# Dealing an adaLN product and half of an output projection over the steps of an attention, and a sum of squares ahead of another adaLN product

## The chip, the core and the metric

One NeuronCore of a Trainium2 chip runs the whole program. The metric is device microseconds per execution, lower is better. All arrays are float32. The engines are TensorE (PE; weight loads are shown apart as PEld), VectorE (DVE), ScalarE (ACT), GpSimd (POOL) and SyncE (SP), which issues the large DMAs.

## The reference

Two residual layers over 256 positions of width 1024. Layer 0 has a mixer of differential and sparse attention, layer 1 a mixer of block attention (8 heads of 64, at this length plain causal attention) beside a diagonal state-space model (S5) with a gated linear unit (GLU). After each mixer comes a mixture of 32 SwiGLU experts. adaLN makes from the vector `c` six rows of 1024 numbers per layer: shift, scale and gate of the mixer, shift, scale and gate of the experts.

```python
mod = c_act @ ada_w[l] + ada_b[l]
sh1, sc1, g1, sh2, sc2, g2 = jnp.split(mod, 6, axis=-1)
h = rms_norm(x) * (1.0 + sc1[:, None, :]) + sh1[:, None, :]
# odd mixer
z = h @ w_in
cq, ck, cv, u = _split(z, ODD_SPLIT)
cq = apply_rope(rms_norm(cq.reshape(bsz, seq, C_HEADS, HEAD_DIM), c_qn), cos_h, sin_h)
ck = apply_rope(rms_norm(ck.reshape(bsz, seq, C_HEADS, HEAD_DIM), c_kn), cos_h, sin_h)
o_c = moba_attention(cq, ck, cv)
y = jax.nn.gelu(s5_scan(u, ...))
y = y * jax.nn.sigmoid(y @ glu_w + glu_b)
y = jnp.concatenate([o_c, y], axis=-1) @ w_out
x = x + g1[:, None, :] * y
h = rms_norm(x) * (1.0 + sc2[:, None, :]) + sh2[:, None, :]
x = x + g2[:, None, :] * hier_moe(h, ...)
```

## The kernel before

Each engine runs one list of instructions, written by hand, and waits on semaphores that the others raise; no scheduler moves anything. The 256 tokens are two tiles `t` of 128. `xT` and `hT` hold the residual and the modulated input with the 1024 features on partitions in 8 blocks `k`; `htok` holds rows by token, and serves as scratch for squares.

All weights come through `ring`, six slots of 2 MB, in one fixed order (`LOADS0`, the 96 expert loads of layer 0, `LOADS1`, 96 expert loads of layer 1). SP issues a load (L439) when the slot's former user has told that it is done, for the mixers through `slot_used`, for the experts through the semaphore of the expert's matmuls.

PSUM has eight banks: `A4` (four), `B4` and `B5` (together `OB`), `B6` and `B7` (`TRB`). Everything that passes through `TRB` is a pass with a name in `ORDER`, PE fills one of the two banks, ACT copies it out (`passed`, `tr_evac`, `ada_evac`), and `pass_bank` makes PE wait for the bank of two passes ago.

An adaLN third `ada{l}r{r}` is 2048 of a layer's 6144 numbers: `ada_part` (L530) multiplies the replicated `crep` (128x32 stationary) with eight half slots of weights, four column groups into the four 32-partition strips of one bank, 32 matmuls in all. A float32 matmul of the program stands as two records in the trace, so a third is 64 records, two `k` of it are 16. ACT copies the bank to `modrow`, and four transposes (`ada{l}c{r}`, L519) and one more copy turn the row into columns `modc`.

The second mixer runs like this on PE: first the half of third 1 (`ada1r1`), the column sums of squares of `xT` (`sum_squares`, L561, into `B5`), the other half. DVE then makes the norm (`norm_modulate`, from L1077 to L1088) and raises `h_ready`. PE projects the S5 input (L983), then `s5_input`, `s5_output` and `project1` (L591) alternate with the scans on DVE. `gated_unit` (L971) fills `B4` and `B5`, ACT makes its sigmoid (L1853, `sig_ready`). `c_norm` on DVE normalizes and rotates q and k of one token tile (it needs a square root from ACT, `root`, L1656) and tells `qk_ready`; the passes `C0` to `C3` (L519) transpose them. Third 2 (`ada1r2`, `ada1c2`) stands between `C1` and `C2`.

`attention` has eight units: `t` 0 and 1, and four pairs of heads each. A step `j` issues the scores of unit j (`att_score`, L606, two 64-row matmuls into half of `A4`), the transposes of its probabilities `LAG_PT` steps later (`att_pt`, L519) and the product with v `LAG_PV` steps later (`att_pv`, L628, into `OB[t]`). DVE scales and masks (L1043), takes the maximum (L1138) and negates it (L1040); ACT exponentiates each of two heads (L1669) and copies the transposed probabilities (L1644). Then `out_proj(1, 1)`, the half of the output projection that takes the S5 rows `hT[:, 4:8]` (DVE L1603, `yo_ready`), fills all of `A4` (L659); `oC0` and `oC1` transpose the attention rows; `out_proj(1, 0)` adds their half, followed block by block by residual, squares and their column sums. The expert stage `moe(1)` begins with the norm, the routing and the packing (L714), then its experts (L742 gate and up, L759 down, L769 combination).

Of the kernel before, what the change touches and what calls it, by code (L numbers as in the profile page):

```python
# [120 lines left out]
def build(nc, a, cst_d, out_d):  # L121
    ctx = ExitStack()
    with ctx:
# [170 lines left out]
        ada_done = sem("ada_rows_done")  # L294
# [82 lines left out]
        LAG_PT, LAG_PV = 3, 4  # L377
# [10 lines left out]
        for j in range(N0 + LAG_PT):  # L388
            if 0 <= j - LAG_PT < N0:
                ORDER.append(f"p{j - LAG_PT}")  # L390
            if j == ADA1_COLS_AT:
                ORDER.append("ada1c0")
        ORDER += ["oB0", "oB1", "oA0", "oA1", "bt0", "bt1", "bt2", "bt3", "ct0", "ct1", "k0", "h0_0", "h0_1", "h0_2", "h0_3", "ada1r1", "ada1c1",
                  "C0", "C1", "ada1r2", "ada1c2", "C2", "C3"]
        ORDER += [f"p{N0 + j}" for j in range(N1)] + ["oC0", "oC1", "h1_0", "h1_1", "h1_2", "h1_3"]
# [101 lines left out]
        def _(pe):  # L497
# [134 lines left out]
            def attention(l, base, units, hook=None):  # L632

                n = len(units)
                for j in range(n + LAG_PV):
                    if j < n:
                        att_score(l, base, j, *units[j])
                    if 0 <= j - LAG_PT < n:
                        att_pt(base, j - LAG_PT, *units[j - LAG_PT])
                    if 0 <= j - LAG_PV:  # L640
                        if l == 1 and j == LAG_PV:
                            pe.wait_ge(sig_ready, 1)
                        if l == 0 and j - LAG_PV in (8, 12):
                            pe.wait_ge(o_ready, (j - LAG_PV) // 4 - 1)
                        att_pv(base, j - LAG_PV, *units[j - LAG_PV])
                    if hook:
                        hook(j)

            def out_proj(l, cc):


                n = n_of(l, "out", cc)
                full(n)
                if cc == 1:
                    pe.wait_ge(score_read, (N0, N0 + N1)[l])
                for b in range(4):
                    for k in range(4):
                        for f in (2 * b, 2 * b + 1):
                            ins = pe.matmul(A4[:, b, TOK * (f % 2):TOK * (f % 2) + TOK],  # L659
                                            slot4(n)[:, k, P * f:P * f + P], hT[:, 4 * cc + k, :],  # L660
                                            start=(cc == 1 and k == 0 and f % 2 == 0), stop=(cc == 0 and k == 3),
                                            skip_group_check=True)
                    if cc == 0:
                        ins.then_inc(wout_done, 1)
                        if b:
                            sum_squares(2 * l + 1, b - 1)
                if cc == 1:
                    ins.then_inc(slot_used, 1)
                else:
                    pe.wait_ge(wout_done, 4 * (l + 1))  # L670
                    pe.nop().then_inc(slot_used, 1)
                    sum_squares(2 * l + 1, 3)
# [241 lines left out]
            for s, name in ((1, "oB"), (0, "oA")):  # L914
# [4 lines left out]
                out_proj(0, s)  # L919
# [9 lines left out]
            pe.nop().then_inc(slot_used, 1)  # L929
# [68 lines left out]
            project1(5)  # L998
            gated_unit()
            for h in range(2):  # L1000
                tr_unit(f"C{h}", [z1[:, 0, 512 * h + P * b:512 * h + P * b + P] for b in range(4)], [(qk_ready, 7)])

            ada_rows(1, 2)
            ada_columns(1, 2)
            for h in range(2):
# [989 lines left out]
```

## Time and profile before

| | before |
|---|---|
| three executions, us | 1469.05, 1465.03, 1468.69 |
| median, us | 1468.69 |
| the profiled execution, us | 1468.64 |
| its span from first to last instruction, us | 1466.8 |
| PE busy, of the span | 1306.7 us, 89% |
| DVE busy | 429.8 us, 29% |
| ACT busy | 217.8 us, 15% |
| mean granted clock of PE | 0.936 of full |

The second mixer lies between 762 and 945 us of the span, the expert stages before and after it. Busy time of PE counts matmuls whose ends are modelled, and a matmul at half clock is busy for longer, so the share alone doesn't say what binds; the idle time before each row and its releaser do.

### The profile page before, as it was taken

Reading aid. Unit: us, or ns where it says so; the run is one execution under the profiler, and the core shown is the slowest. Engines: PE = TensorE matmul, PEld = TensorE weight load, DVE = VectorE, ACT = ScalarE, POOL = GpSimd, SP = SyncE. Lnnn points to the kernel's source line nnn. Section 1 sums busy time; section 2 is a strip of 40 time slices with the busy share of each in tenths; the row PEclk is TensorE's granted clock in tenths of the full one; section 3 lists DMA queues with packets and bytes.
Section 4 is the critical chain, followed back from the end, with each engine's and each line's share of the span. In section 5 each row is a group of like instructions: output and inputs, shape, how many; then the busy total and the mean of one; then the engine's idle time right before and its main releaser. Section 6 shows DMA issues by size and latency. Waiting matters only on the chain.

```text
span 1466.8 us, 15111 instructions
## 1 busy us (share of the span) xinstructions
PE 1306.7 (89%) x6161; PEld 653.0 (45%) x6161; DVE 429.8 (29%) x887; ACT 217.8 (15%) x458; POOL 104.0 (7%) x127
## 2 busy tenths in 40 slices
PE   5999988799898988989978989889989998999897
PEld 2444567643344433433335445664334333343333
DVE  3264567521111110211123954342112111111112
ACT  2121341211110110101010024011101010111110
POOL 2000202100300300300000000000000000000000
PEclk9999859899999999999998997979999999999999
DMA  9987713079999999999998256308999999999993
GB/s 370 379 329 301 275 49 115 0 317 429 428 428 427 427 427 428 428 427 428 428 421 316 113 203 261 115 1 332 427 428 428 428 427 428 427 428 428 428 428 147
DMA packets 51769, 493.45 MB, mean 336 GB/s; under 512 B 4712, under 2 KB 5936, under 8 KB 20848
## 3 DMA queue, kind: packets, MB, share of 16 engines
q1 hardware_dynamic: 48816, 488.33, 80.3%
q10 hardware_dynamic: 1856, 3.20, 0.6%
q0 software_dynamic: 1024, 0.88, 0.3%
q8 instruction: 54, 0.88, 0.2%
q14 instruction: 19, 0.16, 0.0%
HBM read 489.24 MB, written 3.15 MB: 336 GB/s over the span
## 4 chain that ended last, share of the span: by engine, by line
PE 54%; DMA 34%; DVE 7%; issue 3%; ACT 1%; SPq 1%; DVEq 0%; POOLq 0%; POOL 0%; PEldq 0%; ACTq 0%
DMA ring<-in_moe_w 32%; PE B L742 22%; PE B L575 6%; PE B L759 5%; PE A L659 4%; PE B L530 3%; PE A L769 3%; PE B L714 2%; DMA ring<-in_ada_w 2%; PE B L591 2%; PE B L519 1%; PE B L628 1%; PE B L983 1%; DVE hT L1088 1%; PE B L686 1%
## 5 line engine op out<-in xcount | busy, mean ns | idle before, releaser
L742 PE MATMUL B<-ring,work 128*64 128x512 f32 x2048 | 477.6, 621 | 60.0 <-DMA ring<-in_moe_w 57.4
L742 PEld LDWEIGHTS B<-ring,work 128*64 128x64 f32 x2048 | 160.6, 142 | 339.1 <-issue 337.7
L759 PE MATMUL B<-ring,work 128*64 128x512 f32 x1024 | 231.9, 594 | 1.2 <-ACT work L1706 1.2
L1319 DVE TENSOR_TENSOR work<-work,B 64x512 f32<-64x512 f32 x64 | 68.3, 1067 | 496.2 <-ACT work L1702 495.8
L759 PEld LDWEIGHTS B<-ring,work 128*64 128x64 f32 x1024 | 76.6, 137 | 136.6 <-issue 136.6
L1702 ACT ACTIVATE work<-B 64x512 f32<-64x512 f32 x64 | 37.7, 589 | 621.4 <-PE B L742 621.4
L769 PE MATMUL A<-work 128*128 128x256 f32 x512 | 118.1, 384 | 8.9 <-DVE work L1325 8.9
L769 PEld LDWEIGHTS A<-work 128*128 128x128 f32 x512 | 94.7, 190 | 28.4 <-issue 16.9
L1926 POOL COPY work<-work 128x512 f32 x62 | 38.1, 614 | 901.0 <-PE B L742 744.5
L575 PE MATMUL B<-ring,hT 128*128 128x512 f32 (+1 forms) x224 | 94.6, 582 | 4.4 <-DVE hT L1088 3.3
L1325 DVE COPY work<-B 64x512 f32<-64x512 f32 x64 | 43.7, 683 | 117.3 <-PE B L759 117.3
L575 PEld LDWEIGHTS B<-ring,hT 128*128 128x128 f32 x224 | 43.6, 197 | 52.9 <-issue 48.2
L1710 ACT COPY work<-B 64x512 f32<-64x512 f32 x64 | 37.2, 581 | 194.5 <-PE B L759 194.5
L530 PE MATMUL B<-ring,crep 128*32 128x512 f32 x384 | 48.7, 658 | 17.3 <-issue 9.5
L1315 DVE COPY work<-B 128x512 f32<-128x512 f32 x16 | 11.1, 691 | 173.1 <-PE B L733 173.1
L659 PE MATMUL A<-hT,ring 128*128 128x256 f32 x256 | 56.9, 381 | 2.2 <-ACT hT L1644 2.2
L659 PEld LDWEIGHTS A<-hT,ring 128*128 128x128 f32 x256 | 48.3, 190 | 9.3 <-ACT hT L1644 2.9
L749 PEld LDWEIGHTS B<-cst,work 128*128 128x128 f32 x256 | 26.9, 141 | 50.3 <-issue 50.3
L591 PE MATMUL B<-ring,hT 128*128 128x512 f32 x96 | 45.0, 625 | 0.0
L749 PE MATMUL B<-cst,work 128*128 128x128 f32 x256 | 41.9, 286 | 0.0
L714 PE MATMUL B<-work,htok 128*128 128x256 f32 x128 | 33.8, 430 | 8.8 <-DVEq L1046 8.8
L530 PEld LDWEIGHTS B<-ring,crep 128*32 128x32 f32 x384 | 13.5, 119 | 48.3 <-issue 38.9
(251 smaller groups left out, 916.5 us busy)
## 6 DMA issues: line engine op xcount, KB each, us to landing
ring<-in_moe_w SPq DMA_DIRECT2D x192, 2048.0 KB, 19.4
ring<-in_ada_w SPq DMA_DIRECT2D x24, 2048.0 KB, 18.2
ring<-in_ev_w_in SPq DMA_DIRECT2D x6, 2048.0 KB, 11.9
ring<-in_od_w_in SPq DMA_DIRECT2D x4, 2048.0 KB, 16.1
ring<-in_ev_w_out SPq DMA_DIRECT2D x2, 2048.0 KB, 7.6
ring<-in_od_w_out SPq DMA_DIRECT2D x2, 2048.0 KB, 7.6
s_tables<-hT ACTq DMA_DIRECT2D x8, 256.0 KB, 9.6
ring<-s_tables SPq DMA_DIRECT2D x1, 2048.0 KB, 25.5
```

The source lines that it names most:

```text
L530: ins = pe.matmul(bank[32 * g:32 * g + 32, :], crep[:, k, :], slot_rows(n)[:, k % 2, 512 * g:512 * g + 512], start=(k == 0), stop=(k == KD ...
L575: ins = pe.matmul(bank[:, 0:w], hT[:, k, P * t:P * t + P], slot8(n)[:, k, 0:w], start=(k == 0), stop=(k == KD - 1))
L591: ins = pe.matmul(OB[m != 5][:, :], hT[:, k, P * t:P * t + P], slot8(n)[:, k, :], start=(k == 0), stop=(k == KD - 1))
L659: ins = pe.matmul(A4[:, b, TOK * (f % 2):TOK * (f % 2) + TOK], slot4(n)[:, k, P * f:P * f + P], hT[:, 4 * cc + k, :], start=(cc == 1 and k ...
L714: ins = pe.matmul(bank[:, TOK * q:TOK * q + TOK], htok[:, t, P * f:P * f + P], Sp[:, t, TOK * h:TOK * h + TOK], start=(t == 0), stop=(t == 1))
L742: ins = pe.matmul(B5[64 * m:64 * m + 64, :], xs[:, k, :], w[:, k, :], start=(k == 0), stop=(k == KD - 1))
L749: ins = pe.transpose(B6[:, P * k:P * k + P], hid[:, q % 2, P * k:P * k + P], ident)
L759: ins = pe.matmul(B7[64 * m:64 * m + 64, :], hidTb[:, q % 2, k, :], w[:, k, 512 * m:512 * m + 512], start=(k == 0), stop=(k == KF - 1))
L769: ins = pe.matmul(A4[:, f // 2, TOK * (f % 2):TOK * (f % 2) + TOK], y2[:, pr % 2, P * f:P * f + P], SwT[:, g, pr % 2, :], start=False, sto ...
L1319: dve.tensor_tensor(hid[64:128, q % 2, :].rearrange("p (k q) -> p q k", k=KF), silu_a[64:128, q % 2, :].rearrange("p (q k) -> p q k", k=KF ...
L1325: dve.tensor_copy(y2[64 * (q % 2):64 * (q % 2) + 64, (q // 2) % 2, 0:512], B7[0:64, :]).then_inc(sm.y_lo, 1)
L1926: pool.tensor_copy(xge[:, e % 2], xgp[:, :, bass.ds(start, CH)]).then_inc(rows_ready, 1)
```

## The change

Only the second mixer changes.

- `sum_squares(2, b)` stands ahead of the whole of `ada1r1`.
- ACT takes `root(9)` ahead of the copy of projection 4 and `root(10)` ahead of that of projection 5. `C0` and `C1` stand ahead of the gated unit, on PE and on ACT.
- `ada1r2` is no pass through `TRB` any more: it is accumulated in `B5`, two `k` at each of the steps 1 to 4 of the attention, the first after `sig_ready`; ACT copies it at its step 5 (`ada_copied`), and `ada1c2` follows at step 6. The first product into `B5` of the attention (unit 4) waits for that copy.
- The lags of the second attention are 2 and 3 in place of 3 and 4.
- `out_proj` takes one block `b` of output columns a call. Blocks 0 to 2 of `out_proj(1, 1)` stand at the steps 8 to 10 of the attention, behind the last three products with v, block 3 after it. DVE makes `yo_ready` behind unit 5.

```diff
-        LAG_PT, LAG_PV = 3, 4
+        LAGS = [(3, 4), (2, 3)]
+        ADA2_COLS_AT = 6
...
-                        if l == 1 and j == LAG_PV:
-                            pe.wait_ge(sig_ready, 1)
+                        if l == 1 and j - lag_pv == 4:
+                            pe.wait_ge(ada_copied, 1)
...
-            def out_proj(l, cc):
+            def out_proj(l, cc, b, first):
                 n = n_of(l, "out", cc)
-                full(n)
-                if cc == 1:
-                    pe.wait_ge(score_read, (N0, N0 + N1)[l])
-                for b in range(4):
-                    for k in range(4):
+                if b == 0:
+                    full(n)
+                    if first:
+                        pe.wait_ge(score_read, (N0, N0 + N1)[l])
+                for k in range(4):
...
-            bank = pass_bank("ada1r1")
-            ada_part(bank, 1, 1, range(0, 4))
             for b in range(4):
                 sum_squares(2, b)
-            ada_part(bank, 1, 1, range(4, KD))
-            pe.nop().then_inc(tr_done, 1)
-            pe.nop().then_inc(slot_used, 1)
+            ada_rows(1, 1)
...
             project1(5)
+            for h in range(2):
+                tr_unit(f"C{h}", [...], [(qk_ready, 7)])
             gated_unit()
             for h in range(2):
-                tr_unit(f"C{h}", [...], [(qk_ready, 7)])
-
-            ada_rows(1, 2)
-            ada_columns(1, 2)
-            for h in range(2):
                 tr_unit(f"C{2 + h}", [...], [(qk_ready, 8)])
-            pe.wait_ge(tr_ev, U["C3"] + 1)
-            attention(1, N0, L1_UNITS)
-            pe.wait_ge(yo_ready, 1)
-            out_proj(1, 1)
+            pe.wait_ge(tr_ev, U["C1"] + 1)
+            def beside_c(j):
+                if j == 3:
+                    pe.wait_ge(tr_ev, U["C3"] + 1)
+                if 1 <= j <= 4:
+                    if j == 1:
+                        pe.wait_ge(sig_ready, 1)
+                    ada_part(B5, 1, 2, (2 * j - 2, 2 * j - 1))
+                if j == 4:
+                    pe.nop().then_inc(slot_used, 1)
+                if j == ADA2_COLS_AT:
+                    tr_unit("ada1c2", [...], [(ada_copied, 1)])
+                if j >= N1:
+                    if j == N1:
+                        pe.wait_ge(yo_ready, 1)
+                    out_proj(1, 1, j - N1, True)
+            attention(1, N0, L1_UNITS, beside_c)
+            out_proj(1, 1, 3, True)
...
             for j, (s, b, t) in enumerate(L1_UNITS):
                 softmax_unit(16, j, s, b, t, sc_sb1, prob1)
-            dve.wait_ge(gy_ready, 1)
-            dve.wait_ge(sig_ready, 1)
-            dve.tensor_tensor(hT[:, 4:8, :], gy, vv[:, 1], ALU.mult).then_inc(yo_ready, 1)
+                if j == 5:
+                    dve.wait_ge(gy_ready, 1)
+                    dve.wait_ge(sig_ready, 1)
+                    dve.tensor_tensor(hT[:, 4:8, :], gy, vv[:, 1], ALU.mult).then_inc(yo_ready, 1)
...
+            root(9, small[:, 0:16])
             c_evac(4)
-            root(9, small[:, 0:16])
+            root(10, small[:, 0:16])
             c_evac(5)
+            for h in range(2):
+                tr_evac(f"C{h}", qkT1[:, 4 * h:4 * h + 4, 0:P], 4)
             act.wait_ge(in_s5, 16 * N_S5)
             act.wait_ge(glu_done, 1)
             for f in range(4):
                 ins = act.activation(vv[:, 1, f, :], OB[f // 2][...], ACT.Sigmoid, bias=glub[:, f:f + 1])
             ins.then_inc(sig_ready, 1)
             for h in range(2):
-                tr_evac(f"C{h}", qkT1[:, 4 * h:4 * h + 4, 0:P], 4)
-            root(10, small[:, 0:16])
-            ada_evac(1, "r2")
-            ada_evac(1, "c2")
-            for h in range(2):
                 tr_evac(f"C{2 + h}", qkT1[:, 4 * h:4 * h + 4, P:2 * P], 4)
+            def beside_c(j):
+                if j == 5:
+                    act.wait_ge(ada_done, 6)
+                    act.copy(modrow[:, :], B5[:, :]).then_inc(ada_copied, 1)
+                if j == ADA2_COLS_AT:
+                    ada_evac(1, "c2")
```

PE at the start of the second mixer, before (L530 is the adaLN product, L561 the sum of squares, L983 the first projection; a count is one of program matmuls):

```order
L408 COMPARE_AND_BRANCH
L530 MATMUL B<-ring,crep 32x512 x16
L561 MATMUL B<-htok,cst 128x256 x8
L530 MATMUL B<-ring,crep 32x512 x16
L983 MATMUL B<-hT,ring 128x256 x32
L939 MATMUL A<-work,BT 128x128 x16
```

The same place after (the same work has the lines L536, L567 and L985):

```order
L414 COMPARE_AND_BRANCH
L567 MATMUL B<-htok,cst 128x256 x8
L536 MATMUL B<-ring,crep 32x512 x32
L985 MATMUL B<-hT,ring 128x256 x32
L941 MATMUL A<-work,BT 128x128 x16
```

The eight matmuls of the sum of squares moved from the middle of the product to its front; nothing else is different there.

PE from the last projections to the first units of the attention, before (L971 the gated unit, L519 transposes, L606 scores, L628 products with v):

```order
L591 MATMUL B<-ring,hT 128x512 x16
L971 MATMUL B<-work,ring 128x256 x16
L519 MATMUL B<-cst,work 128x128 x8
L530 MATMUL B<-ring,crep 32x512 x32
L519 MATMUL B<-cst,modrow 128x128 x4
L519 MATMUL B<-cst,work 128x128 x8
L606 MATMUL A<-work 128x128 x8
L519 MATMUL B<-cst,work 128x128 x2
L606 MATMUL A<-work 128x256 x2
L519 MATMUL B<-cst,work 128x128 x2
L628 MATMUL B<-work 128x64 x2
```

After (L973, L525, L612, L634 for the same):

```order
L597 MATMUL B<-ring,hT 128x512 x16
L525 MATMUL B<-cst,work 128x128 x8
L973 MATMUL B<-work,ring 128x256 x16
L525 MATMUL B<-cst,work 128x128 x8
L612 MATMUL A<-work 128x128 x4
L536 MATMUL B<-ring,crep 32x512 x8
L612 MATMUL A<-work 128x128 x2
L525 MATMUL B<-cst,work 128x128 x2
L536 MATMUL B<-ring,crep 32x512 x8
L612 MATMUL A<-work 128x128 x2
L525 MATMUL B<-cst,work 128x128 x2
L634 MATMUL B<-work 128x64 x2
```

The transposes of the first token tile went ahead of the gated unit, and the 32 matmuls of the adaLN third became four lots of 8, each behind the scores of a unit.

PE at the end of the attention, before (L659 is the output projection, the last L519 the transposes of the attention rows):

```order
L519 MATMUL B<-cst,work 128x128 x4
L628 MATMUL B<-work 128x64 x4
L519 MATMUL B<-cst,work 128x128 x4
L628 MATMUL B<-work 128x64 x8
L659 MATMUL A<-hT,ring 128x256 x32
L519 MATMUL B<-cst,htok 128x128 x8
```

After (L664 is the output projection):

```order
L525 MATMUL B<-cst,work 128x128 x4
L634 MATMUL B<-work 128x64 x4
L664 MATMUL A<-hT,ring 128x256 x8
L525 MATMUL B<-cst,work 128x128 x4
L634 MATMUL B<-work 128x64 x4
L664 MATMUL A<-hT,ring 128x256 x8
L634 MATMUL B<-work 128x64 x4
L664 MATMUL A<-hT,ring 128x256 x16
L525 MATMUL B<-cst,htok 128x128 x8
```

The last two products with v now stand between blocks of the output projection, and the last half of it stands between the last product and the transposes of the rows.

## Rows read from the trace of the kernel before

**Rows 1.** The page, part 4: chain of work that ended last.

```profile
PE 54%; DMA 34%; DVE 7%; issue 3%; ACT 1%; SPq 1%; DVEq 0%; POOLq 0%; POOL 0%; PEldq 0%; ACTq 0%
```

**Rows 2.** Windows: stretch, length, busy time by engine, PEclk, DMA share, GB/s.

```profile
774.00:776.00 2.00, 2.00 (x12) 0.46 (x8) 0.00 (x0) 0.00 (x0) 0.00 (x0) 0.50 1.07 415
776.00:778.00 2.00, 2.00 (x17) 0.50 (x10) 0.00 (x0) 0.00 (x0) 0.00 (x0) 0.79 1.05 430
...
790.00:792.00 2.00, 2.00 (x7) 1.60 (x6) 1.93 (x4) 0.00 (x0) 0.00 (x0) 0.62 1.05 386
...
880.00:882.00 2.00, 2.00 (x12) 0.44 (x8) 1.05 (x2) 0.88 (x2) 0.00 (x0) 0.50 1.00 414
...
890.80:896.80 6.00, 4.48 (x25) 2.46 (x25) 4.02 (x12) 4.14 (x14) 0.00 (x0) 0.67 1.00 384
896.80:906.80 10.00, 9.89 (x40) 7.20 (x40) 6.96 (x14) 5.40 (x21) 0.00 (x0) 0.51 0.89 378
906.80:911.70 4.90, 4.85 (x41) 4.59 (x42) 1.29 (x3) 2.71 (x7) 0.00 (x0) 1.00 0.01 5
...
944.70:983.20 38.50, 27.46 (x128) 24.50 (x129) 24.92 (x81) 7.26 (x11) 0.00 (x0) 0.69 0.12 49
983.10:1450.00 466.90, 432.83 (x1966) 182.87 (x1968) 71.36 (x97) 51.19 (x98) 19.04 (x31) 0.97 0.96 405
```

**Rows 3.** Timeline, PE at the start of the mixer: start, us, work, idle before.

```profile
771.85 6.09 PE L530 MATMUL B<-ring,crep 128*32 128x512 f32 x32 [9.47 <-issue]
777.87 3.72 PE L561 MATMUL B<-htok,cst 128*128 128x256 f32 x16
781.52 3.64 PE L530 MATMUL B<-ring,crep 128*32 128x512 f32 x32
...
789.65 15.77 PE L983 MATMUL B<-hT,ring 128*128 128x256 f32 x64 [4.49 <-DVE hT L1088]
```

**Rows 4.** Timeline, DVE in the same stretch.

```profile
770.61 0.69 DVE L1060 TENSOR_TENSOR htok<-xT 128x512 f32<-128x512 f32 x1
...
781.71 0.42 DVE L1077 TENSOR_SCALAR rstd<-B 128x256 f32<-128x256 f32 x1 [10.32 <-PE B L561]
```

**Rows 5.** Timeline, PE from the last projections to the attention.

```profile
851.89 15.70 PE L591 MATMUL B<-ring,hT 128*128 128x512 f32 x32
868.30 7.14 PE L971 MATMUL B<-work,ring 128*128 128x256 f32 x32 [0.72 <-ACT work L1841]
875.75 1.06 PE L519 MATMUL B<-cst,work 128*128 128x128 f32 x8 [0.30 <-PE B L971]
878.92 8.77 PE L530 MATMUL B<-ring,crep 128*32 128x512 f32 x64 [2.11 <-ACT work L1644]
888.49 0.66 PE L519 MATMUL B<-cst,modrow 128*128 128x128 f32 x4 [0.80 <-ACT modrow L1648]
...
890.80 0.71 PE L606 MATMUL A<-work 64*128 64x128 f32 x8 [0.68 <-ACT work L1644]
```

**Rows 6.** Timeline, ACT in the same stretch.

```profile
862.65 0.22 ACT L1656 ACTIVATE small<-small 128x16 f32<-128x16 f32 x1
...
875.54 1.28 ACT L1853 ACT_TABLE_LOAD   x1 [7.33 <-PE B L971]
876.83 1.57 ACT L1853 ACTIVATE work<-B,glub 128x256 f32<-128x256 f32 x4
```

**Rows 7.** Timeline, DVE: q and k of tile 1, then units 4, 5, 7.

```profile
881.21 1.22 DVE L1037 TENSOR_TENSOR work<-work,small 128x1024 f32<-128x1024 f32 x1
...
897.07 0.69 DVE L1043 SCALAR_TENSOR_TENSOR work<-A,cst 128x512 f32<-128x512 f32 x1 [0.23 <-DVE small L1040]
...
899.07 0.69 DVE L1043 SCALAR_TENSOR_TENSOR work<-A,cst 128x512 f32<-128x512 f32 x1 [0.27 <-PE A L606]
...
904.11 0.69 DVE L1043 SCALAR_TENSOR_TENSOR work<-A,cst 128x512 f32<-128x512 f32 x1 [0.79 <-PE A L606]
```

**Rows 8.** Timeline, PE at the output projection.

```profile
911.62 14.03 PE L659 MATMUL A<-hT,ring 128*128 128x256 f32 x64
```

More of the change, by code:

```diff
@@ L646, in attention @@
                     if hook:
                         hook(j)
-            def out_proj(l, cc):
+            def out_proj(l, cc, b, first):
                 n = n_of(l, "out", cc)
-                full(n)
-                if cc == 1:
-                    pe.wait_ge(score_read, (N0, N0 + N1)[l])
-                for b in range(4):
-                    for k in range(4):
[L658 to L667, printed above, removed]
+                if b == 0:
[3 more added lines that the diff above has]
+                for k in range(4):
+                    for f in (2 * b, 2 * b + 1):
+                        ins = pe.matmul(A4[:, b, TOK * (f % 2):TOK * (f % 2) + TOK],
+                                        slot4(n)[:, k, P * f:P * f + P], hT[:, 4 * cc + k, :],
+                                        start=(first and k == 0 and f % 2 == 0), stop=(not first and k == 3),
+                                        skip_group_check=True)
+                if not first:
+                    ins.then_inc(wout_done, 1)
+                    if b:
+                        sum_squares(2 * l + 1, b - 1)
+                    if b == 3:
+                        pe.wait_ge(wout_done, 4 * (l + 1))
+                        pe.nop().then_inc(slot_used, 1)
+                        sum_squares(2 * l + 1, 3)
+                elif b == 3:
@@ L918, in _ @@
                 pe.wait_ge(tr_ev, U[f"{name}1"] + 1)
[L919 removed]
+                for b in range(4):
+                    out_proj(0, s, b, s == 1)
             s5_transposes()
             moe(0)
[L923 to L924 removed]
             for b in range(4):
                 sum_squares(2, b)
[L927 to L929 removed]
+            ada_rows(1, 1)
             pe.wait_ge(h_ready, 6)
@@ L1013, in _ @@
             pe.wait_ge(tr_ev, U["oC1"] + 1)
-            out_proj(1, 0)
+            for b in range(4):
+                out_proj(1, 0, b, False)
             moe(1)
@@ L1678, in att_pt, with attention @@
                 tr_evac(f"p{base + j}", pt[:, (base + j) % 2, 0:nb, :], nb)
-            def attention(base, units, buf, pr, pt, hook=None):
-                n = len(units)
-                for j in range(n + LAG_PT):
+            def attention(l, base, units, buf, pr, pt, hook=None):
+                n, lag_pt = len(units), LAGS[l][0]
+                for j in range(n + lag_pt):
                     if 0 <= j - 1 < n:
                         att_exp(base, j - 1, *units[j - 1], buf, pr)
-                    if 0 <= j - LAG_PT:
-                        att_pt(base, j - LAG_PT, *units[j - LAG_PT], pt)
+                    if 0 <= j - lag_pt:
+                        att_pt(base, j - lag_pt, *units[j - lag_pt], pt)
                     if hook:
@@ L1814, in ada1 @@
                     ada_evac(1, "c0")
-            attention(0, L0_UNITS, sc_sb, prob, PT, ada1)
+            attention(0, 0, L0_UNITS, sc_sb, prob, PT, ada1)
             for t in range(TT):
```

47 lines of the change are left out of this document (26 added, 21 removed).

## Prediction

> **What bounds the kernel now.** I read the chain of waits first: PE carries 54% of the span, DMA 34%, DVE 7% [rows 1]. The DMA share lies in the expert stages, so the first question is whether time won in the second mixer reaches the end at all. In the windows table, the stretch from 944.7 to 983.2 us (norm, routing, packing) moves nearly nothing: DMA share 0.12. From 983.1 to 1450 it is 0.96 at 405 GB/s [rows 2]. The six slots of the ring are full before the second expert stage, and the stream goes on only when the first expert gives its slots back. So the stage is tied to the moment at which PE reaches the first expert, and what the mixer ends earlier, the program ends earlier, one for one.
>
> Then the timeline of the mixer. At its start PE begins at 771.85; DVE has had the squares ready since about 771.3 but gets the column sums only at 781.7, as the first half of an adaLN product stands ahead of them; PE then waits 4.49 us for the norm [rows 3, 4]. From 851.89 on the engines take turns: projections, gated unit, 2.11 us for ACT, the adaLN third of 8.77 us, three more handovers, then the attention from 890.8 [rows 5]. In the attention the windows show the thing to see: 4.48 of 6.0 us busy, then 9.89 of 10.0 but at a granted clock of 0.51 [rows 2]. PE looks full there and runs at half speed, on short work of which it has little. After it come 14.03 us of output projection at full clock [rows 8].
>
> **Part A, sum of squares first.** PE still starts at 771.85, which "issue" ended [rows 3], and the last squares are done by then [rows 4]. The clock is at half until 776.8: the window from 776 to 778 has 0.79, which puts the rise there, and the one before has 0.50 [rows 2]. The sums cost 3.72 us at full clock [rows 3]. In the 4.98 us at half they get through 2.49 of it, the other 1.23 follow at full: end at 778.1 instead of 781.6. The norm starts 3.5 us earlier.
>
> The whole adaLN product now lies beside the norm: twice 3.64 us [rows 3], 778.1 to 785.4. The norm with its modulation takes from 781.71 to 789.65 [rows 3, 4], so PE is released at 786.15 and the product is covered with 0.7 us to spare. Without that cover each us sticks out as it is. The idle time of PE shrinks from 4.49 to 0.7 us. Before, the clock fell behind it: 0.62 in 790 to 792 [rows 2], and L983 took 15.77 us for 64 records [rows 3], where the same shape takes 14.03 at full clock [rows 8]. I take this loss of 1.7 us as gone. Together **5.2 us**. The bounds of that second term are 0 and 1.7; I take the upper, since PE is idle for less than it is in places that keep full clock, as the 0.72 us ahead of the gated unit [rows 5]. The loads behind the third's slots (three projection weights) are issued up to 6 us later, 20 us ahead of their use: nothing. The stage with the scans moves as it is; its short clock dips can come or go, up to 1.7 us either way (the size of the one above).
>
> **Part B, from the projections through half the output projection.** All times here are in the trace's own count, so part A comes off on top. The projections end at 867.6 [rows 5].
>
> Square root 9 on ACT ran at 862.65, behind a projection's copy [rows 6]. Ahead of it, the norm of tile 0 ends some 3 us earlier, in front of 867.6, and root 10 needn't wait for the sigmoid: the three large products of tile 1 (1.22 us each), which began at 881.21 [rows 7], fall beside the gated unit. One ACT table load less; this all is off PE's path. C0 and C1 (1.06 us), gated unit (7.14), C2 and C3 (1.06) [rows 5] with small gaps end at 877.5, and the scores of units 0 and 1 need only C0 and C1, copied long before. Before, scores began at 890.8. The sigmoid with its table load takes 1.28 and 1.57 us after the gated unit [rows 6], until 879.1, and the first lot of the third waits for that behind the scores of unit 1: 0.9 us of wait. What is queued behind it are the scores of unit 2 and the transposes of unit 0; DVE, with two units in hand, hardly feels it.
>
> From 877.5 on PE has to do, at full clock:
> - the third: 2 x 3.64 = 7.3 us [rows 3]; its column transposes 0.7 [rows 5];
> - half the projection: 14.0 [rows 8];
> - the attention's own work: 4.85 us in the stretch at 1.00, half of 9.89 = 4.9 in the one at 0.51, and 4.48 x 0.67 = 3.0 in the first [rows 2], together 12.8.
>
> That is 34.8 us. Waits on top: 0.9 for the sigmoid; 1.7 for one short fall of the clock around the sigmoid (before, 880 to 882 was at 0.50 after a similar pause [rows 2]); 1.6 at the transposes of unit 6, because DVE makes units with 256 keys every 2.0 us when it needn't wait (897.07 to 899.07 [rows 7]) and the 1.22-us product for the S5 rows now stands between units 5 and 6. The lag is one step shorter, but a step of PE is 2 to 3 us, about what DVE and ACT take for one unit. Sum: 877.5 + 34.8 + 4.2 = 916.5. I keep 0.4 for the self-waits of the third and of C3: 916.9. The three steps with unit 5 to 7 hold only light work, like the stretch that fell to 0.51. There I take one short fall, another 1.7 us: 918.6, against 925.7 = 911.62 + 14.03 [rows 8]. **7.1 us.** Its bounds: 8.8 without the fall, 4.0 if the clock stays low for the whole of these steps (the 6 us that they need double, minus the wait of 1.6 that this swallows and the 1.7 already counted, so 3.1 more).
>
> What stays late next: the transposes of the attention rows. Their last product with v is done 7 us before the projection half ends, DVE's scaling takes under 1 us of it, so they are ready, as before. The expert weights that take the third's slots are issued later by a few us, and are needed 60 us later: nothing.
>
> A rule of the skill speaks against the dealing: four lots instead of one switch the array between tile shapes (128*32, 64*128, 128*128) eight times more. The rows at such a switch, L530 to L561 and back, start at 777.87 and 781.52 while the former's modelled end is 777.94 and 781.59 [rows 3]: no gap to be seen. The Trainium skill (TensorEngine Tiling (Array Packing), Key Properties) says that a change of tiling mode drains the engine. It gives no price; going by the rows I put it at nothing, going by the page the gain would be smaller by eight drains.
>
> **Sum.** 5.2 + 7.1 = 12.3 us. From the profiled execution's own 1468.64 that is **1456.3 us**; the median of the three runs is the same within 0.1, though one of them was 3.7 us lower. A measurement of this kernel can tell about 0.3%, 4.4 us, from no change.
>
> **The rivals.**
>
> *The clock holds better* than I assume: no fall in the last steps, and one dip less in the scan stage. 1468.64 - 5.2 - 8.8 - 0.9 (half a dip) = 1453.7. For it: PE is nearly without gaps. Against: it was without gaps at 0.51 as well [rows 2].
>
> *The clock stays at half through the last steps of the attention*, until the projection's blocks have run for some us: B is 4.0, the time 1459.4. For it: 9.89 of 10.0 us busy did not lift the clock [rows 2]. Against: the third's lots, which ran up from 0.50 to full at the mixer's start [rows 2, 3], now stand right before, and blocks of 3.5 us right behind. The Trainium skill (TensorE: Matmul & The Clock Gate, Part 4: PE-mode transpose) has a rule with this result: transposes don't count as busy for the clock. By that rule, the trace agrees as far as the stretch at 0.51 goes, in which transposes are one part of three.
>
> *The cover in part A fails*: with 32-column tiles the clock falls back, the product takes up to 14.6 us from 778.1, ends at 792.7, and L983 starts 3.1 us later than before. Then A is -3.1 and the time 1468.64 + 3.1 - 7.1 = 1464.6. Against: at 781.52 the same tiles ran at 1.00.
>
> *Slower than before*: the mixture never lifts the clock, from the first lot of the third to the end of the projection half. All 34.8 us take twice that, 877.5 + 69.6 = 947.1 against 925.7, so +21.4 - 5.2 = +16.2: 1484.8. It decides the sign once some 14 of the 34.8 us (12.3 and the 1.7 already allowed) run at half. Against: both the third and the projection are dense blocks which stood at full clock [rows 3, 8].
>
> *The gain is not passed on* by the expert stage, as its transfers would be late anyway: no change. Against: share 0.12 in the 38 us before it [rows 2].
>
> **Chances.** Forecast 0.50 (1455 to 1458); clock holds better 0.19; half clock in the last steps 0.20; cover fails 0.04; slower 0.03; not passed on 0.02; 0.02 for something between the last ones. The range takes the first three and their bounds: a clock without any fall at all gives about 1452, the low case with a dip more 1461. Faster by over 0.3% is 0.92 (the first three and part of the others), within 0.3% 0.05, slower 0.03.
>
> **What would show it.** After: the norm's first DVE instruction near 778; PE's wait before the first projection under 1 us, and that projection near 14.1 us; scores of unit 0 at about 872 (877.5 - 5.2); the projection half of the S5 rows ending near 913; granted clock over 0.8 between, with the dip in the steps 5 to 8; the expert stage as long as before. The forecast is wrong if that stage is longer than before, if PE waits for exponentials at every step (the shorter lag), or if the clock between 872 and 913 is below 0.75.

## The result, and the profile after

| | before | after |
|---|---|---|
| median, us (4 executions each) | 1466.86 | 1451.88 |
| lowest to highest | 1464.02 to 1469.05 | 1449.95 to 1453.35 |
| the profiled execution | 1468.64 | 1451.21 |
| its span | 1466.8 | 1449.4 |
| granted clock of PE | 0.936 | 0.947 |

The ratio is 0.9895, 95% interval 0.9873 to 0.9917, so about 15 us less. The forecast was 1456.3, 12.3 us less. The sign is right, but the size is too small, and the time lies just under the lower end of the range (about 1452). The two profiled executions differ by 17.4 us; the one of before, from which the forecast started, was 1.8 us above the median of its kernel.

The timeline of PE after, at the start of the mixer (start, us, work, idle before), answers to [rows 3]:

```profile
772.84 5.92 PE L567 MATMUL B<-htok,cst 128*128 128x256 f32 x16 [9.54 <-DVE htok L1077]
778.69 7.07 PE L536 MATMUL B<-ring,crep 128*32 128x512 f32 x64
786.82 14.08 PE L985 MATMUL B<-hT,ring 128*128 128x256 f32 x64 [1.06 <-DVE hT L1105]
```

The sums come first, the whole third runs in one piece beside the norm, PE waits 1.06 us for the norm in place of 4.49, and the first projection takes 14.08 us in place of 15.77. In this execution everything began 0.93 us later than in the one of before: the last combination of the first expert stage started at 759.61, where it had started at 758.68.

From the gated unit to the output projection, which answers to [rows 5, 8]:

```profile
862.75 1.06 PE L525 MATMUL B<-cst,work 128*128 128x128 f32 x8 [0.30 <-PE B L597]
863.65 7.07 PE L973 MATMUL B<-work,ring 128*128 128x256 f32 x32
871.02 1.06 PE L525 MATMUL B<-cst,work 128*128 128x128 f32 x8 [0.30 <-PE B L973]
872.02 0.72 PE L612 MATMUL A<-work 64*128 64x128 f32 x8
873.72 1.92 PE L536 MATMUL B<-ring,crep 128*32 128x512 f32 x16 [0.99 <-ACT work L1875]
875.58 0.49 PE L612 MATMUL A<-work 64*128 64x128 f32 x4
...
892.45 0.66 PE L525 MATMUL B<-cst,work 128*128 128x128 f32 x4 [1.08 <-ACT work L1688]
892.95 1.08 PE L634 MATMUL B<-work 128*128 128x64 f32 x8
893.87 3.67 PE L664 MATMUL A<-hT,ring 128*128 128x256 f32 x16
...
903.00 7.13 PE L664 MATMUL A<-hT,ring 128*128 128x256 f32 x32
```

The scores begin at 872.0, the wait for the sigmoid is 0.99 us, the one before the transposes of unit 6 is 1.08 us, and the half projection ends at 910.1. The window over all of it (columns as in [rows 2]) shows what differs most from before, the clock:

```profile
872.00:910.00 38.00, 34.82 (x238) 24.67 (x238) 13.35 (x30) 15.61 (x50) 2.94 (x4) 1.00 0.73 281
```

PE is busy for 34.82 us of it, which is what the forecast had added up (34.8), and never at less than full clock.

For the experiments I count from the end of the last combination of the first expert stage (762.37 before, 763.30 after), as the start of that instance moves by some us from execution to execution. All points are read from the timelines of PE, in one traced execution per kernel. Two traces of the kernel before differ by up to 0.8 us at a point, so differences of that size say nothing.

| kernel | first projection starts | projections end | first scores | half projection ends | first expert starts |
|---|---|---|---|---|---|
| before | 27.3 | 105.2 | 128.4 | 163.3 | 220.8 |
| before_again | 26.9 | 104.4 | 127.6 | 162.5 | 220.1 |
| changed | 23.5 | 99.1 | 108.7 | 146.8 | 203.8 |
| sums_first | 23.8 | 99.4 | 121.0 | 160.5 | 217.8 |
| sums_between | 27.2 | 105.1 | 114.7 | 152.8 | 210.4 |
| c_first | 27.4 | 105.4 | 124.1 | 163.9 | 221.2 |
| third_late | 26.9 | 104.3 | 123.7 | 162.8 | 220.2 |
| order_late | 26.8 | 104.3 | 113.9 | 152.8 | 210.1 |
| sums_first_proj_dealt | 23.8 | 99.4 | 120.9 | 157.3 | 214.4 |
| third_whole | 23.2 | 98.8 | 108.4 | 146.4 | 203.5 |
| proj_whole | 23.4 | 99.1 | 108.7 | 147.4 | 204.4 |
| both_whole | 23.7 | 99.4 | 109.0 | 150.6 | 207.7 |
| lags_3_4 | 23.8 | 99.5 | 109.1 | 146.9 | 204.2 |

The change brings the first expert of the second stage 17.0 us nearer, and the span is shorter by 17.4 (with the 0.93 that it started late, what follows the start of that expert gave 1.3 more). What the mixer ends earlier, the program ends earlier, as forecast.

### The profile page after: what moved, and what is told of

Read it like the earlier page. It is cut to its first block, busy times and chain, and to the rows that moved or that the text cites. A ratio compares the mean times of both kernels' runs of the same rounds, so it can differ in the third digit from the quotient of the medians.

```text
span 1449.4 us, 15110 instructions
## 1 busy us (share of the span) xinstructions
PE 1294.3 (89%) x6161; PEld 648.2 (45%) x6161; DVE 430.7 (30%) x887; ACT 216.4 (15%) x457; POOL 104.3 (7%) x127
## 4 chain that ended last, share of the span: by engine, by line
PE 51%; DMA 35%; DVE 8%; issue 2%; ACT 1%; SPq 1%; DVEq 0%; POOLq 0%; POOL 0%; PEldq 0%; ACTq 0%
DMA ring<-in_moe_w 34%; PE B L747 22%; PE B L581 7%; PE B L764 4%; PE A L664 4%; PE A L774 2%; PE B L719 2%; PE B L536 2%; DMA ring<-in_ada_w 2%; PE B L525 1%; PE B L597 1%; PE B L985 1%; PE B L634 1%; DVE hT L1105 1%; PE B L691 1%
## 5 line engine op out<-in xcount | busy, mean ns | idle before, releaser
L664 PE MATMUL A<-hT,ring 128*128 128x256 f32 x256 | 57.4, 381 | 2.2 <-ACT hT L1663 2.2
L664 PEld LDWEIGHTS A<-hT,ring 128*128 128x128 f32 x256 | 48.2, 190 | 9.2 <-ACT hT L1663 2.9
L536 PE MATMUL B<-ring,crep 128*32 128x512 f32 x384 | 44.8, 612 | 5.8 <-DMA ring<-in_ada_w 4.2
L754 PEld LDWEIGHTS B<-cst,work 128*128 128x128 f32 x256 | 26.9, 141 | 50.3 <-issue 50.3
L719 PEld LDWEIGHTS B<-work,htok 128*128 128x128 f32 x128 | 26.8, 212 | 14.7 <-issue 10.4
```

What stands on the lines that cost most here:

```text
L536: ins = pe.matmul(bank[32 * g:32 * g + 32, :], crep[:, k, :], slot_rows(n)[:, k % 2, 512 * g:512 * g + 512], start=(k == 0), stop=(k == KD ...
L719: ins = pe.matmul(bank[:, TOK * q:TOK * q + TOK], htok[:, t, P * f:P * f + P], Sp[:, t, TOK * h:TOK * h + TOK], start=(t == 0), stop=(t == 1))
L754: ins = pe.transpose(B6[:, P * k:P * k + P], hid[:, q % 2, P * k:P * k + P], ident)
```

## Experiments

My theory was: part A is worth its 5 us by itself, and part B pays because dense work dealt over the steps keeps the clock up. The rivals were that the parts depend on each other, and that the order of the work ahead of the attention pays and not the dealing.

### The two parts apart

`sums_first` is the kernel before with this alone:

```diff
-            bank = pass_bank("ada1r1")
-            ada_part(bank, 1, 1, range(0, 4))
             for b in range(4):
                 sum_squares(2, b)
-            ada_part(bank, 1, 1, range(4, KD))
-            pe.nop().then_inc(tr_done, 1)
-            pe.nop().then_inc(slot_used, 1)
+            ada_rows(1, 1)
```

> The kernel before with one edit, the sums of squares ahead of the adaLN third. Theory (dealing keeps the clock up, the sums are worth their own 5 us): PE waits about 1 us for the norm in place of 4.5, the first projection takes 14.1 us in place of 15.8, the mixer is 5 us shorter up to there; the attention stays as it was, 20 to 21 us with granted clock 0.5 to 0.6 in its second half; time 4 to 6 us under before. Rival (most of the gain comes from here, since a fall of the clock less changes all that follows): the attention too holds a clock above 0.8, time over 8 us under before.

Measured: ratio 0.9972 (0.9961 to 0.9983), 4 us under before. The trace agrees with the theory up to the projections, 5.8 us nearer, even 7.4 at the first scores, as the adaLN third ahead of them takes 7.07 us in place of 8.77. Then 4.7 us are given back, 3.6 in the attention and 1.1 in the half projection (15.18 us in place of 14.03). So the attention did not stay as it was, and there the expectation was wrong. The windows of the attention, first of this kernel, then of a second execution of it:

```profile
883.40:907.80 24.40, 22.55 (x105) 17.86 (x105) 12.27 (x27) 12.25 (x41) 0.00 (x0) 0.56 0.63 251
```

```profile
881.80:906.30 24.50, 22.56 (x105) 17.90 (x105) 12.27 (x27) 12.30 (x41) 0.00 (x0) 0.56 0.62 247
```

and of the kernel before, in the execution of [rows 2] and in another:

```profile
890.80:911.60 20.80, 19.12 (x104) 14.15 (x105) 12.27 (x27) 12.26 (x41) 0.00 (x0) 0.67 0.72 294
```

```profile
890.40:911.20 20.80, 19.11 (x104) 14.11 (x105) 12.27 (x27) 12.28 (x41) 0.00 (x0) 0.67 0.71 289
```

DVE and ACT do the same in both (12.27 us). PE is at a mean clock of 0.56 in place of 0.67 and needs 24.4 us in place of 20.8. It repeats from execution to execution, so it belongs to the kernel:

> The kernel before, unchanged, for a second trace. If the stretch at half clock in the attention belongs to the kernel, it is 13 to 14 us again, within a step of 3.4; if it depends on the execution, it can be 20 to 24 us, and the half projection then ends up to 5 us later, counted from the end of the experts.

> The kernel with the sums first alone, for a second trace. First trace: 23.9 us at half clock, half projection ends 160.5 us after the last combination of the experts, where before has 163.3. If that stretch varies by execution, this trace can show 13.7 us at half and an end near 156.

Single executions, 1468.36 and 1462.84 us. Both give the pattern of the first trace again (the half projection of `sums_first` ends at 160.6 in the table's count, where the first trace has 160.5), so for these two kernels nothing speaks for a pattern that changes with the execution.

`sums_between` is the changed kernel with the diff above taken back.

> The changed kernel with that one edit taken back: the sums of squares stand again in the middle of the adaLN third. Theory: PE waits 4.5 us for the norm and the clock falls at the first projection, 15.8 us; the attention with dealt work holds full clock; time 5 us over the changed kernel, 10 us under before. Rival: the parts depend on each other, and the attention falls to half clock, time within 4 us of before.

Measured: ratio 0.9933 (0.9916 to 0.9950), 9.8 us under before; the attention at full clock, as the theory had it:

```profile
877.20:915.30 38.10, 34.94 (x239) 24.83 (x239) 13.62 (x30) 15.56 (x50) 2.93 (x4) 1.00 0.72 280
```

But alone the parts bring the first expert 3.0 and 10.4 us nearer, together 17.0. 3.6 us exist only together, as much as the attention of `sums_first` is longer than before at its lower clock. With part B in place, whose attention stays at full clock, the sums bring 6.6 us.

### Taking the dealing back

In `third_whole` the adaLN third stands in one piece at step 1:

```diff
-                if 1 <= j <= 4:
-                    if j == 1:
-                        pe.wait_ge(sig_ready, 1)
-                    ada_part(B5, 1, 2, (2 * j - 2, 2 * j - 1))
-                if j == 4:
+                if j == 1:
+                    pe.wait_ge(sig_ready, 1)
+                    ada_part(B5, 1, 2, range(KD))
                     pe.nop().then_inc(slot_used, 1)
```

> The changed kernel, but the adaLN third stands in one piece at step 1 of the attention, behind the sigmoid; the projection is still dealt. Theory A (what keeps the clock up is the dense adaLN work inside each step): the steps 2 to 7 hold attention work alone again and run at a granted clock of 0.5 to 0.7, the half projection ends 4 to 6 us later than in the changed kernel. Theory B (the clock was low before only because PE came to the attention with pauses and the lag made it wait): the steps stay at 1.00, the end moves by less than 2 us, by what DVE and ACT can't make meanwhile.

In `proj_whole` all four blocks of the half projection stand behind the attention (`for b in range(4): out_proj(1, 1, b, True)` after the wait for `yo_ready`), and `both_whole` has both edits.

> The changed kernel, but the half projection stands whole behind the attention; the third is still dealt. Theory A and B both: the last steps lose their filler, PE waits 1 to 2 us more in all for exponentials and copies at the steps 8 to 10, and the projection starts after the last product with v. Theory A expects one fall of the clock there (3.4 us at half, 1.7 us lost), in all 3 to 4 us over the changed kernel; theory B 1 to 2 us.

> The changed kernel with nothing dealt: the adaLN third in one piece at step 1 of the attention, the half projection whole behind it; order of C0 and C1, roots, lags and sums as changed. Theory A (dense work inside each step holds the clock): the steps 2 to 10 fall to a granted clock of 0.5 to 0.6 and take 18 us as before the change, 5 to 8 us over the changed kernel. Theory B (the clock isn't tied to it): clock 1.00, 2 to 4 us over.

Measured: 1450.98, 1451.43 and 1452.06 us; ratios 0.9884 (0.9867 to 0.9900), 0.9891 (0.9872 to 0.9911) and 0.9889 (0.9867 to 0.9910), all as the changed kernel. Theory A is wrong for each alone: the third in one piece costs nothing (first expert 203.5 against 203.8), the projection in one piece 0.6 us, which is within what two traces of one kernel differ by. With both whole, the trace fits neither theory: the clock is not low through the steps, but it falls once near their end, and the half projection ends 3.7 us later. Windows of `both_whole`, from the attention's third step on:

```profile
882.80:895.60 12.80, 10.60 (x80) 8.09 (x80) 9.79 (x21) 8.20 (x31) 0.78 (x2) 1.00 1.01 378
895.60:902.40 6.80, 6.48 (x27) 5.94 (x27) 1.51 (x4) 1.61 (x5) 0.00 (x0) 0.50 0.85 360
902.40:915.30 12.90, 12.90 (x62) 11.30 (x61) 0.00 (x0) 0.00 (x0) 0.00 (x0) 1.00 0.00 0
```

12.8 us of bare attention at full clock, then 6.8 at half, across the last products and the first of the projection. Whether the fall belongs to this kernel or to this execution stays open: the traced execution took 1456.75 us and is the slowest of four, while the other three (1449.2, 1451.47 and 1452.66) lie where the changed kernel lies. So in the changed kernel, too, the times give the dealing no gain.

`lags_3_4` is the changed kernel with `LAGS = [(3, 4), (3, 4)]`, all four blocks at the steps 8 to 11.

> The changed kernel with the old lags of 3 and 4 in the second attention. If the shorter lag matters: one more step before the last product, in which only a block of the projection stands, so nothing is lost there, but PE's wait of 1.08 us at the transposes of unit 6 is gone: within 1 us of the changed kernel, either way. Rival (the shorter lag itself removed PE's waits): 3 us or more over the changed kernel.

Measured: 1450.74 us, ratio 0.9896 (0.9870 to 0.9922); the first expert at 204.2 against 203.8. In the changed kernel the shorter lag is worth nothing that can be seen.

### The order ahead of the attention

`c_first` is the kernel before with both square roots, C0 and C1 ahead as in the change. `third_late` is the kernel before with only the third moved, in one piece, to step 1.

> The kernel before with one edit: both square roots on ACT ahead of the copies behind which they stood, C0 and C1 ahead of the gated unit. The adaLN third still stands between C1 and C2. Theory (this order alone is worth a little; the gain sits in the third behind the first scores): the 2.11 us for which PE waits ahead of the third go, and the scores begin 2 to 3 us earlier, counted from the end of the projections; the attention keeps its half clock and its 34.9 us; time 2 to 3 us under before. Rival (the order is what pays): 6 us or more.

> The kernel before with one edit: the adaLN third in one piece in the other bank, behind the sigmoid and behind the scores of units 0 and 1; lags 3 and 4, projection whole, C0 and C1 behind the gated unit, sums in the middle, all as before. Theory: DVE and ACT work through the first two units beside the third, the handovers around it (2.11 and 0.80 us) are gone, PE comes to the attention's steps with units in hand and the clock stays at full for most of them; counted from the end of the projections to the end of the half projection 48 to 51 us in place of 58.1. Rival (dealing is needed): over 54 us, the clock at half in the steps.

Measured: ratios 0.9998 (0.9983 to 1.0012) and 0.9994 (0.9978 to 1.0011). Neither gains anything, where 2 to 3 us were expected of the first and 7 to 10 us up to the half projection of the second. In `c_first` the scores begin 4.3 us earlier, counted as in the table, and the attention and the half projection (15.36 us in place of 14.03) eat it, the attention at a clock of 0.56:

```profile
889.20:913.50 24.30, 22.20 (x104) 17.67 (x105) 12.26 (x27) 12.24 (x41) 1.56 (x3) 0.56 0.75 289
```

In `third_late` the attention's steps behind the third are at full clock (units with 256 keys take 0.70 us for their scores, not 1.23), but PE waits ahead of them. Its timeline, C0 and C1, then C2 and C3:

```profile
876.40 1.06 PE L525 MATMUL B<-cst,work 128*128 128x128 f32 x8 [0.30 <-PE B L977]
885.78 1.97 PE L525 MATMUL B<-cst,work 128*128 128x128 f32 x8 [8.31 <-DVEq L1063]
```

and DVE meanwhile:

```profile
881.57 0.25 DVE L1136 RECIPROCAL small<-small 128x16 f32<-128x16 f32 x1 [11.09 <-ACT small L1674]
```

C2 and C3 need q and k of tile 1. Their norm waits 11 us for root 10, which stands behind the sigmoid on ACT. Before, the third covered this; moved behind the scores, it lays the wait bare. I had missed that: this run's expectation is wrong by it. The two together:

> The kernel before with the two edits of order together: square roots, C0 and C1 ahead, and the adaLN third in one piece behind the scores of units 0 and 1. Lags, projection and sums as before. Theory (they need each other: the early roots make q and k of tile 1 ready, for which PE otherwise waits 8.3 us once the third no longer covers it): the end of the half projection comes 7 to 10 us earlier, counted from the end of the experts, with a short stretch at half clock at the end of the attention; time 6 to 9 us under before. Rival (dealing is what pays): under 3 us.

Measured: 1458.21 us, ratio 0.9927 (0.9906 to 0.9947), 10.7 us under before. Up to the half projection it gains 10.5 us, more than the 7 to 10 expected and without the stretch at half clock, as much as `sums_between` (both 152.8), with lags 3 and 4 and nothing dealt. So with the sums in the middle, all of part B is these two moves of order, each of which gains nothing alone. The window of its attention from the third step to the projection:

```profile
885.00:900.90 15.90, 13.19 (x100) 10.23 (x101) 10.25 (x21) 9.81 (x34) 0.60 (x2) 1.00 1.01 390
```

The last one asks what the dealt projection does where the clock is low:

> The kernel with the sums first, and the half projection dealt over the last four steps of the attention, all else as before. Theory (dense blocks among the light steps lift the clock): the clock rises with the first block, so that the stretch at half ends some 5 us earlier than with the sums first alone, and the last three products with v run at full clock; half projection 4 to 5 us earlier, time 7 to 8 us under before. Rival (one block between light work isn't enough): no change against the sums first alone, 3 to 4 us under before.

Measured: ratio 0.9949 (0.9932 to 0.9965), 7.5 us under before, against 4 for `sums_first` (the intervals of the two overlap slightly). In the trace the half projection ends 3.2 us earlier than there (157.3 against 160.5), less than the 4 to 5 expected. Its timeline around the first block:

```profile
902.21 1.97 PE L628 MATMUL B<-work 128*128 128x64 f32 x8
903.97 4.70 PE L660 MATMUL A<-hT,ring 128*128 128x256 f32 x16
908.50 0.60 PE L519 MATMUL B<-cst,work 128*128 128x128 f32 x4
908.94 1.00 PE L628 MATMUL B<-work 128*128 128x64 f32 x8
```

The block begins at half clock (4.70 us in place of 3.67), and from then on a product with v takes 1.00 us in place of 1.97. Here the clock rises under a single dealt block, and so some us earlier than in `sums_first`, where it rises under the whole projection behind the attention.

### The idle time at the start, and a version beyond the change

In the traces of both kernels PE is idle for 9.5 us between the first expert stage and the second mixer. Between them stands a loop of three rounds for experts with over 64 tokens, whose rounds do nothing on these inputs. `one_branch` is the changed kernel with:

```diff
-            with eng.Fori(0, MORE) as c:
-                with eng.If(c < extra):
+            with eng.If(extra > 0):
+                with eng.Fori(0, MORE) as c:
+                    with eng.If(c < extra):
```

> The changed kernel with one more test around the loop that handles experts with over 64 tokens (none here), so that each engine passes the whole loop with one branch in place of three rounds. Theory: the 9.5 us that PE is idle with nothing to wait for, ahead of the sum of squares, are the branches of that loop over its long body. With one branch PE is there before the squares are, the sums end 4 to 5 us earlier and PE's idle time is under 5 us; the end of the program gains too, in all 5 to 8 us under the changed kernel. Rival (the idle time is the load of the count, or the fetch of the code behind the loop): idle time stays 9 us, within 1 us of the changed kernel.

> The changed kernel with the transposes of the attention rows ahead of the last block of the half projection, which then covers ACT's copies. The wait of 0.72 us ahead of the second half projection goes, if DVE's scaling of the rows is done when PE comes (it has 3.5 us for less than 1 us of work, after the last product with v, only if the block before covers it: it doesn't, the last product stands directly ahead of block 2): 0.7 us shorter up to the norm, in the times within noise.

> The changed kernel with both edits that gained in the trace: one branch around the loop for large experts, and the transposes of the attention rows ahead of the last block of the projection. Theory: they add up, 10.8 and 1 us under the changed kernel, 1439 to 1441 us. Rival: the second is eaten by a fall of the clock as in other stages, 1441 to 1442 us.

> The kernel before with the one branch around the loop for large experts. With the half adaLN product ahead of the sums, PE starts when the branch is through, about 3 us after the last combination of the experts in place of 9.5, and the sums end 6 us earlier; then 1.5 to 3 us from the end of the program: 8 to 10 us under before. Rival (in this order the loads of the adaLN weights, which land at about 770, then hold PE up): only 3 to 5 us under before.

`one_branch`: 1441.07 us, ratio 0.9824 (0.9801 to 0.9847), 10.8 us under the changed kernel (10.4 by the two ratios), the lowest median of all, and more than the 5 to 8 expected. PE's timeline there:

```profile
758.52 3.69 PE L775 MATMUL A<-work 128*128 128x256 f32 x16 [0.82 <-DVE work L1343]
765.50 5.41 PE L568 MATMUL B<-htok,cst 128*128 128x256 f32 x16 [3.29 <-DVE htok L1078]
770.84 7.07 PE L537 MATMUL B<-ring,crep 128*32 128x512 f32 x64
```

The idle time is 3.29 us and is ended by the squares, the first projection starts 6.8 us earlier than in the changed kernel, counted as in the table. At the first expert it is 6.9 us; another 1.7 lie at the end of the program, behind the last combination of the experts, where the changed kernel still takes 11.6 us and this one 9.9. `rows_early` moves `oC0` and `oC1` ahead of block 3 of the half projection: the wait of 0.72 us ahead of the second half is gone and the last column sums ahead of the norm start 0.8 us nearer, as expected, but the first expert is at 203.7 against 203.8, and the time is 1451.85, so nothing that times resolve. Both edits together gave 1441.71 (0.9837, 0.9811 to 0.9862), not better than the branch alone, though the first expert comes at 196.0 against 196.9. `before_one_branch` gave 1462.43 (0.9965, 0.9951 to 0.9978), 5 us under before and not the 8 to 10 expected: the scores begin 7.3 us nearer, the half projection ends only 1.2 us nearer. As in `sums_first`, the gain is lost where the clock is low: the attention takes 24.7 us at a mean clock of 0.61 (before 20.8 at 0.67), the half projection 16.22 (before 14.03). Its rival (weights landing late) is not the reason, as the third started with 3.66 us of idle time.

## Why the prediction was wrong, and what in it was right

- **The step that failed.** It is the clock in part B. I added two falls of 1.7 us each. One, around the sigmoid, I took from 880 to 882 us before, at 0.50 after a similar pause; the other, in the steps 5 to 7, from the stretch at 0.51, whose work is as light. There was none: the granted clock is 1.00 from 872 to 910 us. The time that came is that of the range's lower end, "a clock without any fall at all". The case "the clock holds better", which I gave 0.19, still kept the fall at the sigmoid. Of the 5.1 us by which the traced execution is below the forecast, 3.3 lie in part B, 0.9 in part A and 0.9 behind the half projection and in the start; the median lies 0.7 above that execution.
- **That the gain reaches the end.** Right: 17.0 us at the first expert, 17.4 in the span.
- **Part A, 5.2 us.** In the changed kernel 6.1 us up to the end of the projections, with its small terms: the norm earlier (sums end at 778.8, forecast 778.1 and 0.93 for the late start), the wait 1.06 for 0.7, the projection 14.08 for 14.03, the scan stage 0.6 slower, the last projections 1.2 faster. The last two lie within the dips that I had left open. But I wrote of it as a sum of its own, and that was wrong: alone it is worth 3.0 us, and only in front of the changed part B all of it.
- **Part B, 7.1 us.** Measured 10.4, from 58.1 to 47.7 between the end of the projections and that of the half projection. The work (34.8 forecast, 34.82 measured) was right. The waits were right in sum (2.9 forecast with the self-waits, 3.3 measured), partly by balance: the one for the sigmoid was 0.99 us for 0.9 and the one at unit 6 was 1.08 for 1.6, but one of 0.81 us for ACT, at the transposes of unit 0 (start 876.88), I had not foreseen. The mis-sized term is the clock, 3.4 us forecast and nothing measured, which is the whole miss of part B.
- **Why the clock holds.** I gave the dense work between the steps as the reason why the clock might hold. The runs show that it isn't needed: with everything whole the clock still held for 12.8 us of attention, and in `order_late` for all of it. So light work alone doesn't bring the clock down, and the stretch at 0.51 was no measure for the same work in another order.
- **Two sums.** The bound 4.0 of part B doesn't follow from its own terms: 6 less 1.6 and 1.7 is 2.7 and not 3.1, which gives 4.4 and puts the low rival at 1459.0. And where I wrote that 14 us at half would decide the sign, two falls of 1.7 had been allowed, so it is 15.7. Neither changes the forecast.
- **Rivals.** Half clock in the last steps is what the same edits give without the rest (`c_first`, `sums_first`), so its 0.20 was not far-fetched; in the changed kernel it did not come. The lost cover and the slower case did not come. No shift was swallowed by the expert stage.
- **Tiling modes.** After the change, L536 from 873.72 for 1.92 us is followed by L612 at 875.58, another tile shape, with no gap. The drain at a change of tiling mode, of which the Trainium skill tells (TensorEngine Tiling (Array Packing), Key Properties), has no price that a row shows here: of the 3.2 us in which PE is idle between 872 and 910, 2.9 are waits for ACT.

What stays open: why the clock falls in one order and not in the other. The runs show which orders do it, not the rule. They also don't part the dense third behind the first scores from the waits that went with its move.

## What to carry to other kernels

Where a stretch of light work runs at half clock, time won ahead of it can be given back inside it: check the clock of the following stage before adding an edit's gain to a sum, and try edits together that need each other, because two that gain nothing alone gave 10.7 us here. A dense block of work for which nobody waits can stand right behind the first small pieces of a chain between engines, but first ask what it had covered where it stood. And look at idle time that no wait explains between stages: one test around a loop that has nothing to do on these inputs was worth 10.8 us on top of the change's 15, though only 5 in the kernel before.

## What the hardware showed that I had not expected

- Nearly the same instructions of the same attention ran at a clock of 1.00 with PE busy for 83% (13.19 of 15.9 us in `order_late`), and at 0.50 with PE busy for 98%, in `sums_first` (the last 2.2 us of this window are the half projection already):

```profile
886.20:910.00 23.80, 23.25 (x97) 18.51 (x95) 11.64 (x26) 10.13 (x36) 0.00 (x0) 0.50 0.53 219
```

  So the busy share in these stretches does not tell their clock. What differs is what came before: in `order_late` 7.08 us of adaLN product behind the first scores, in `sums_first` waits of 0.36 and 0.94 us between the first three. That this is the cause is not shown. Without the transposes PE is busy for 8.35 of 15.9 us in `order_late` (13.19 less 4.84) and for 16.20 of 23.8 in `sums_first` (23.25 less 7.05). The rule that I had named for the low case (the Trainium skill, TensorE: Matmul & The Clock Gate, Part 4: PE-mode transpose) is that transposes don't count as busy in the same way. It doesn't tell these two stretches apart: the one with the smaller share of other work has the full clock.
- The pattern of the clock repeated from one execution to the next in the two kernels that were traced twice (0.67 twice before, 0.56 twice in `sums_first`).
- With three empty rounds of a loop with a long body PE was idle for 9.5 us; with one branch around the loop for 3.3, the last part of which is a wait for DVE.
